# A hybrid S5 / short-convolution / expert-retrieval step on one core: the front's DVE and TensorE orders, its loads, and the latents' query weights rearranged

## The reference

```python
sh1, sc1, g1, sh2, sc2, g2 = modulation(cond)                # silu(cond) @ w_mod + b_mod, once for each of the two conditions
h = rmsnorm(x, norm1_g) * (1 + sc1) + sh1
u, cb, cc, ch = split(h @ w_in)
y_ssm  = gelu(s5_scan(u, forward) + s5_scan(u, backward) + d_skip * u); y_ssm *= sigmoid(y_ssm @ w_glu + b_glu)
y_conv = cb * short_conv(cc * ch)                            # width 3
x = x + g1 * (concat(rmsnorm(y_ssm), rmsnorm_by_head(y_conv)) @ w_out)
h = rmsnorm(x, norm2_g) * (1 + sc2) + sh2
for each block of 128 tokens, for each of 8 heads:
    q = h @ w_query[head]                                    # 256 columns
    s = q halves @ sub_keys                                  # 2 x 128 scores for a token
    idx, top = 16 best of the sums of the 16 best of each half
    out += (gelu(expert_u[idx] . h) * softmax(top)) @ expert_v[idx]
x = x + g2 * out;  y = rmsnorm(x, final_norm_g)
```

## Time and profile before

| | |
|---|---|
| median of 3 runs | 1988.73 us (1987.07 to 1994.5) |
| the profiled execution's own time | 1987.85 us |
| its span | 1986.1 us |
| busy PE / DVE / ACT / POOL | 1201.5 / 1443.9 / 375.6 / 736.0 us |
| moved by DMA | 745.90 MB, 671.13 of them by POOL's queue |
| first expert row set issued at | 234.18 us |

### The profile page before, as it was taken

How to read it: one execution, slowest core, us unless ns; L and a number is a source line. 1 busy time by engine, 2 the same in 40 slices (tenths; PEclk the granted TensorE clock), 3 DMA queues, 4 the chain that set the end, 5 groups by cost and what they waited for, 6 DMA issues and landing times.

```text
span 1986.1 us, 22255 instructions
## 1 busy us (share of the span) xinstructions
PE 1201.5 (60%) x7540; PEld 465.5 (23%) x7540; DVE 1443.9 (73%) x3889; ACT 375.6 (19%) x845; POOL 736.0 (37%) x673
## 2 busy tenths in 40 slices
PE   5988988888867666666544443364344454444444
PEld 2557733333322222222111000021000011111001
DVE  8778367877766776766788777777777767877675
ACT  4241342122222221111111110121011111211110
POOL 3100132333433333343443444444444444344442
PEclk8999989999968877777655555575555556555555
DMA  8556499999989999999999999999999999999996
GB/s 337 170 186 209 155 394 383 358 394 389 395 339 390 382 393 394 401 403 388 421 421 420 415 417 413 421 407 414 416 415 420 409 414 410 416 421 404 415 414 258
DMA packets 126098, 745.90 MB, mean 376 GB/s; under 512 B 12112, under 2 KB 34896, under 8 KB 40352
## 3 DMA queue, kind: packets, MB, share of 16 engines
q0 software_dynamic: 92160, 671.13, 82.8%
q1 hardware_dynamic: 33824, 73.35, 10.5%
HBM read 741.78 MB, written 2.65 MB: 375 GB/s over the span
## 4 chain that ended last, share of the span: by engine, by line
DMA 31%; PE 29%; DVE 26%; issue 10%; ACT 2%; POOL 0%; DVEq 0%; POOLq 0%; SPq 0%; ACTq 0%
DMA r<-table,gidx 30%; DVE r L1675 8%; PE bank L843 7%; PE bank L811 6%; PE bank L920 3%; PE bank L931 2%; DMA r<-w_query 1%; DVE wgt L1687 1%; PE bank L778 1%; DVE r L1643 1%; DVE i L1617 1%; PE bank L539 1%; PE bank L638 1%; DVE i L1623 1%; DVE r L1618 1%
## 5 line engine op out<-in xcount | busy, mean ns | idle before, releaser
L1875 POOL DMA_INDIRECT r<-table,gidx x640 | 708.9, 1108 | 1063.9 <-PE bank L843 902.6
L1675 DVE CUSTOM_DVE_ANT_0 r<-r 128x1024 f32<-128x1024 f32 x640 | 779.9, 1224 | 310.9 <-DMA r<-table,gidx 292.3
L843 PE MATMUL bank<-r,wgt 128*32 128x512 f32 x2560 | 536.6, 923 | 727.7 <-DVE wgt L1687 709.0
L843 PEld LDWEIGHTS bank<-r,wgt 128*32 128x32 f32 x2560 | 61.4, 130 | 1102.7 <-DVE wgt L1687 1032.2
L1223 ACT ACTIVATE r<-r 128x2 f32<-128x2 f32 x320 | 65.1, 203 | 1045.7 <-DVE r L1675 1042.8
L811 PE MATMUL bank<-hT_r,r 128*128 128x512 f32 x256 | 120.4, 625 | 0.9 <-ACT hT_r L1079 0.9
L1684 DVE TENSOR_TENSOR r<-r 128x2 f32<-128x2 f32 x320 | 50.2, 157 | 82.0 <-ACT r L1223 82.0
L1687 DVE TENSOR_TENSOR wgt<-fold,r 128x64 f32<-128x64 f32 x320 | 72.0, 225 | 11.1
L811 PEld LDWEIGHTS bank<-hT_r,r 128*128 128x128 f32 x256 | 50.3, 202 | 75.9 <-issue 75.9
L1223 ACT ACT_TABLE_LOAD x51 | 65.4, 1283 | 0.9
L920 PE MATMUL bank<-hT_r,r 128*128 128x512 f32 x128 | 62.9, 636 | 0.0
(11 more groups left out here) (362 smaller groups left out, 1472.6 us busy)
## 6 DMA issues: line engine op xcount, KB each, us to landing
r<-w_mod SPq DMA_DIRECT2D x24, 1024.0 KB, 7.8
r<-w_query SPq DMA_DIRECT2D x15, 1024.0 KB
r<-table,gidx POOLq DMA_INDIRECT x640, 11.6
r<-w_tiles SPq DMA_DIRECT2D x12, 512.0 KB, 8.1
x_r<-w_tiles SPq DMA_DIRECT2D x10, 512.0 KB, 4.9
hT_r<-xT SPq DMA_DIRECT2D x4, 640.0 KB, 6.3
r<-w_u SPq DMA_DIRECT2D x1, 2048.0 KB, 31.3
r<-w_o SPq DMA_DIRECT2D x1, 2048.0 KB, 10.5
```

The source lines that it names most:

```text
L843: last = mm(bank[ACC[b % 2][h]][to:to + TG, :], wgt[:, g % 2, e, :], rows[:, k % SLOTS, D + h * 512:D + (h + 1) * 512], start=(G % HEADS = ...
L1675: V.tensor_tensor_reduce(rows[:, s, 0:D], rows[:, s, 0:D], h2r[tg], 1.0, 0.0, ALU.mult, ALU.add, hid[:, par, k:k + 1]).then_inc(dot_done, 1)
L1875: G_.indirect_dma_start(rows[:, k % SLOTS, :], None, table, bass.IndirectOffsetOnAxis(gidx[:, e, k:k + 1], 0)).then_inc(row_in[k % SLOTS], 16)
```

## The change

It moves work in the front and gives the latents' query weights another load and PE another order.

- `bcs` is loaded in two halves: B ahead of the slabs, C (semaphore `ld_cc`) behind `w_u`.
- DVE: `chunk_inputs(0)` goes ahead of the norm's inversion, the gains go between the fourth and fifth scaled tile, and all eight groups of CP are DVE's. POOL's group of CP is gone, and its Bd copies wait for CP.
- PE: turns 0 to 3 go between the slabs 5, 6 and 7, turns 4 to 7 behind the second u tile (turns 4 to 7 stood behind the fifth). Slabs 20 and 21 go behind the two halves of L625, slab 22 ahead of the context's outputs. ACT takes turns 0 to 3 out ahead of the modulation rows.
- DVE's lag blocks come one scan step earlier.
- SP: the first two convolution tiles use the two buffers that the gate's weights need, so that the gate's weights are loaded after two tiles and not after six; the first query's weights go behind two tiles, and `w_o` goes ahead of the last two.
- Latents' queries: `load_query` ends with context head 7. `load_query_lat(n)`, n = 0 and 1, loads the weights of four heads at once as eight loads of 512 KB (one for each k, pieces of 4 KB) into `wq4`, spread over pairs by waits on the count of gelus. `query_lat` of heads u = 9 to 15 is cut in quarters of four matmuls, behind the pairs g = 2, 3 (h = 0) and 4, 5 (h = 1), the scores behind g = 6; for u = 8 whole halves go behind g = 5 and 6 and the scores ahead of g = 7. ACT's copies follow the gelus of g = 4 and 6 (u = 8: 6 and 7), and g = 7 for the scores.

```diff
             def load_conv_ctx(q):
                 if q >= 6:
-                    sp.wait_ge(zc_mm, (1, 2, 3, 4, 7, 8)[q - 6])
+                    sp.wait_ge(zc_mm, q - 3)
...
+            def load_query_lat(n):
+                if n:
+                    sp.wait_ge(lq_mm, HEADS)
+                for k in range(KD):
+                    if n == 0 and k:
+                        sp.wait_ge(gelu_done, NPR * (HEADS - 3) + 6 + k)
+                    elif n and k % 2 == 0 and k:
+                        sp.wait_ge(gelu_done, NPR * (HEADS + 1) + 6 + k // 2)
+                    sp.dma_start(wq4[k // KS][:, k % KS, :], w_query[:, k, 4 * DQ * n:4 * DQ * (n + 1)]).then_inc(ld_wq0, 16)
...
+                if n == 46:
+                    sp.wait_ge(zol_mm, KD)
+                    sp.wait_ge(q_mm, HEADS)
+                    load_query_lat(0)
+            sp.wait_ge(out_ready, 1)
+            sp.dma_start(y_out[:, :, 0:P], peer.rearrange("p (k t) -> p k t", k=KD)).then_inc(out_dma, 16)
+            load_query_lat(1)
...
+                elif h == 0:
+                    pe.wait_ge(ld_wq0, 16 + 16 * KD * (n + 1))
...
-                    if HEADS <= u < NQC:
-                        if g in (4, 5):
-                            query_lat(u, g - 4)
+                    if u == HEADS and g == 7:
+                        scores_lat(u)
+                    add_rows(G, g)
+                    if u == HEADS:
+                        if g in (5, 6):
+                            query_lat(u, g - 5, range(KD))
+                    elif HEADS < u < NQC:
+                        if g in (2, 3, 4, 5):
+                            query_lat(u, g // 4, range(4 * (g % 2), 4 * (g % 2) + 4))
                         if g == 6:
                             scores_lat(u)
-                    add_rows(G, g)
...
                     if HEADS <= u < NQC:
-                        if g in (4, 5):
-                            take_q_lat(u, g - 4)
-                        if g == 6:
+                        if g in ((6, 7) if u == HEADS else (4, 6)):
+                            take_q_lat(u, int(g > 4 + 2 * (u == HEADS)))
+                        if g == 7:
                             take_scores_lat(u)
```

More of the change, by code:

```diff
@@ L395, in _ @@
                 sp.dma_start(hT[:, 2 * j:2 * j + 2, :], xT[:, 2 * j:2 * j + 2, :]).then_inc(ld_x[j], 16)
-            sp.dma_start(bcs, bc).then_inc(ld_bc, 16)
+            sp.dma_start(bcs[:, 0:2], bc[:, 0:2]).then_inc(ld_bc, 16)
             for n in range(8):
@@ L399, in _ @@
             sp.dma_start(wu, w_u).then_inc(ld_wu, 16)
+            sp.dma_start(bcs[:, 2:4], bc[:, 2:4]).then_inc(ld_cc, 16)
             sp.dma_start(dsk[0:NCH, :], dskip).then_inc(ld_dsk, 16)
@@ L406, in _ @@
             sp.wait_ge(d_mm, 1)
-            for q in range(4):
+            for q in range(2, 6):
                 load_conv_ctx(q)
             sp.wait_ge(us_mm, 2)
-            for q in range(4, 6):
+            for q in range(2):
                 load_conv_ctx(q)
@@ L413, in _ @@
                 load_mod(n)
-            for q in range(6, 10):
+            sp.wait_ge(zc_mm, 2)
+            for j in range(2):
+                sp.dma_start(wt[:, j, :, :], w_tiles[NCONV + j]).then_inc(wtg_in, 16)
+            for q in range(6, 8):
                 load_conv_ctx(q)
@@ L417, in _ @@
             sp.dma_start(wqa, w_query[:, :, 0:DQ]).then_inc(ld_wq0, 16)
[L418 to L421, removed]
+            for q in range(8, 10):
                 load_conv_ctx(q)
@@ L424, in _ @@
             sp.dma_start(woA, w_o[:, 0:4, :, :]).then_inc(ld_woa, 16)
+            for q in range(10, 12):
+                load_conv_ctx(q)
             sp.wait_ge(zc_mm, 10)
@@ L462, in _ @@
                     load_out_lat(n - 30)
-                if n % NPR == 5:
+                if n % NPR == 5 and n // NPR + 3 < HEADS:
                     load_query(n // NPR + 3)
[L465 to L469, removed]
+                if n == 46:
[5 more added lines that the diff above has]
+            load_query_lat(1)
             for b in range(1, NBLK - 1):
@@ L533, in turn_input @@
                 last.then_inc(bpt_mm, 1)
+            pe.wait_ge(silu_done, 1)
+            for n in range(KD):
+                mod_slab(n)
+                if n in (5, 6):
+                    turn_input(2 * (n - 5))
+                    turn_input(2 * (n - 5) + 1)
+            mod_turn(0)
             def u_lat(k):
@@ L558, in _ @@
                 mod_slab(KD + k)
-                if k in (1, 4):
-                    for e in range(4):
-                        turn_input((0 if k == 1 else 4) + e)
+                if k == 1:
+                    for e in range(4, 8):
+                        turn_input(e)
             pe.wait_ge(bpt_ev, 7)
@@ L627, in _ @@
                 last.then_inc(m_mm, 1)
[L628 to L629 removed]
+                mod_slab(20 + a)
+            mod_slab(22)
             def conv_ctx(r):
@@ L809, in query_lat @@
                     pe.wait_ge(topk_done, u)
-                for k in range(KD):
-                    last = mm(bank[2 + h][:, :], wqb[:, k, h * P:(h + 1) * P], hT[:, k, CTX:T], start=(k == 0), stop=(k == KD - 1))
-                last.then_inc(lq_mm, 1)
+                for k in ks:
+                    last = mm(bank[2 + h][:, :], wq4[k // KS][:, k % KS, at:at + P], hT[:, k, CTX:T], start=(k == 0), stop=(k == KD - 1))
+                if ks[-1] == KD - 1:
+                    last.then_inc(lq_mm, 1)
             def scores_lat(u):
@@ L1100, in mod_take @@
                       bank[6 + h][:, CW:CW + 16].rearrange("p (m a c) -> p a m c", m=MCH, a=4), ACT.Copy).then_inc(mod_free, 1)
+            for e in range(4):
+                take_input(e)
             mod_rows(0)
@@ L1108, in _ @@
                 modulate(0, k, 1, CTX, T).then_inc(h_ready, 1)
-            for e in range(8):
+            for e in range(4, 8):
                 take_input(e)
@@ L1426, in _ @@
             V.tensor_copy(sv[:, 9, :], sv[:, 4, :]).then_inc(bb_ready, 1)
-            dve.wait_ge(rms_act, 2)
-            link(V.reciprocal(rs, rs))
-            for k in range(KD):
-                tt(hT[:, k, :], hT[:, k, :], rs, ALU.mult).then_inc(xs_ready, 1)
             def chunk_inputs(n):
@@ L1455, in _ @@
             chunk_inputs(0)
-            gains(1, COL_N1, 2)
+            dve.wait_ge(rms_act, 2)
+            link(V.reciprocal(rs, rs))
+            for k in range(KD):
+                if k == 4:
+                    gains(1, COL_N1, 2)
+                tt(hT[:, k, :], hT[:, k, :], rs, ALU.mult).then_inc(xs_ready, 1)
             for n in range(1, 4):
@@ L1460, in _ @@
             ct = tv.rearrange("p (q j c) -> p q j c", q=4, j=Q + 1)
-            for q4 in range(CP_POOL, NQ, 4):
+            dve.wait_ge(ld_cc, 16)
+            for q4 in range(0, NQ, 4):
                 q = slice(q4, q4 + 4)
```

55 lines of the change are left out of this document (14 added, 41 removed).

## The result

The changed kernel takes **1999.75 us** (median, 1998.43 to 2002.36) against 1988.3 us for the kernel before (1987.07 to 1994.5) in the same session: ratio **1.0049, interval 1.003 to 1.0069**. The forecast was 1966 us, range 1952 to 1984. The change is slower, by about as much as a measurement of this kernel can just tell, and the forecast missed by 34 us. The profiled execution has a span of 1998.8 us.

What follows compares the result with a forecast made beforehand. It took a PE, DVE and ACT relay to bound the front until 234 us, then the DMA engines: 1987.85 - 13.8 (front) - 8.8 (queries) = 1965.2, plus 0.9 for the median, 1966 us; range 1952 to 1984.

Steps and rivals of the forecast that it cites:

- The front: All before the first expert row set, a relay between PE, DVE and ACT: -10.1 - 3.7 = -13.8 us; ends -7 and -17.
- (a) to (c): Front: u starts 4.5 us sooner, PE reaches chunk states at 102.6, CP ready at 98.6, first copy out 10.1 us sooner.
- (e): Gate weights loaded after two tiles: PE's 2.81 us wait goes, L713 starts 3.8 us sooner; -3.7 us.
- The load of 8 MB in 4 KB pieces: Latents' query weights: 2.7 us for 1 MB against 3.1 in 1 KB pieces; eight heads gain 3 us.
- late loads: Rival: PE's first latent query waits for its group's loads, stopping POOL and DMA; 2007 us if landing takes 29.7; chance 0.06.
- the row that priced it at 29.7 us: Profile row of the load at 397.84, in 1 KB pieces, which took 29.67 us and held PE up.
- a wait for `w_query` of more than 3 us: Sign named in advance that the prediction is wrong: PE waiting this long for the query weights.
- The step of u = 8: First latents' query step, keeping whole bursts: loses 9.6 us in place of 5.1, 4.5 us later than now.
- The 16.0 us of waiting: Rest of the 8 latents' query steps, 365.4 - 324.6 - 8 x 3.1; forecast to fall to 13.1 us.
- 324.6 us of row sets: The 8 latents' query steps at 40.6 us each for 16 row sets, the base before loads and waiting.
- ACT's wait: Latents' query steps: ACT's gelu stands behind PE's burst, DVE waits 32.2 us in 11 times; quarters end it.
- 171 forecast: DMA engines: price in ns of one 4 KB piece, so 2.7 us for 1 MB.

Runs made afterwards that it cites:

- e1: The changed kernel's front alone, with the query loads, PE's query order and ACT's takes of the kernel before; 1978.27 us, ratio 0.995.
- e3: The changed kernel with its four-head loads, but PE's whole query bursts and ACT's copies in the places of the kernel before; 1989.12 us, ratio 0.9997.
- e4: The changed kernel with no gelu waits in the second group's loads and y_out stored behind them; 1991.71 us, ratio 1.0022.
- e6: Against e1: no loads of the latents' query weights, the queries use head 7's (output not the reference's); 1973.52 us, ratio 0.9927.
- e7: Against e1: latents' queries of two matmuls for a half instead of eight, loads kept (output not the reference's); 1955.93 us, ratio 0.9848.
- e9: Against e1: both no loads of the latents' query weights and two matmuls of eight for each query half; 1939.58 us, ratio 0.9756.
- e8: Against e1: one-head 1 MB loads into two buffers in turn, all latents' queries in quarters, ACT's takes one pair later; 1973.41 us, ratio 0.9925.
- e5: The changed kernel with the first group's eight loads issued in one go and u = 8's query in quarters; 1995.15 us, ratio 1.0035.
- e10: Against e8: from u = 9, each query's first half moved behind pairs 7 and 0, weights loaded one head further ahead; 1966.89 us, ratio 0.9891.

## Why the prediction was wrong

- *The front*: (a) to (c) right: 4.45 us at u (4.5), 7.5 at the chunk states (6.8), CP at 98.1 (98.6), the first copy out 10.6 sooner (10.1). DVE's scan behind it starts even 12.0 sooner, 114.99 in place of 126.94, because before, PE still had 96 of its 128 matmuls to do after that copy, and now it goes straight through. (e) is too large: PE's wait for the gate weights is gone, but it now waits 6.35 us behind the gate for ACT, and the output projection starts at 181.36 in place of 194.10, 12.7 sooner. So (e) gave under 1 us and not 3.7. The first row set is 12.8 sooner for 13.8 because the two errors nearly cancel. In the medians e1 shows 9.9 of it, 6.8 to 12.9. Timelines of DVE and PE after:

```profile
114.99 0.20 DVE L1539 COPY fin<-r 128x64 f32<-128x64 f32 x1 [9.28 <-ACT r L1168]
170.98 1.84 PE L691 MATMUL bank<-ones,mix_r 128*128 128x1 f32 x8 [6.35 <-ACT mix_r L1193]
181.36 2.02 PE L763 MATMUL bank<-mix_r,r 128*128 128x128 f32 x16 [0.76 <-issue]
```

- *The load of 8 MB in 4 KB pieces.* The step that failed: I took the landing of one 512 KB load, 9.1 us, for that of the last of eight. A single load does land in that time (8.64 us in e3's chain); the last of eight queued within 13 us lands in 29.24 in the changed kernel (32.20 in e4, where they are queued within 4), and q1 has little over a quarter of the engines meanwhile. I had the right rival, late loads with a threshold of about 20 us, and the row that priced it at 29.7 us, and gave it 0.06. I put that row aside because it was in 1 KB pieces; it would have given the right time for the second group. By that rival both groups would be late; the first is paced over 36 us in place of 13, its last load lands like a lone one, and it was late only in e3. Of the 41 us that the rival had for both groups, one wait of 15.21 us came; it is also the sign that I had named, a wait for `w_query` of more than 3 us. And I had no term at all for four heads' weights in one step: e3 shows some 7 us of it.
- *The step of u = 8*: I had it 4.5 us longer, it was 9.2. Ahead of it the head start is 10.9 us, and 14.5 in e1, but that is no price of the loads: e6, which loads no weights for the latents, has 8.7. Of this, 3.6 us arise between the spreads at about 408 and 460 us, where the programs of e1 and e6 are the same, and a context query waits 2.59 us for its weights and then runs at 3.52 us in e6, 1.51 and 2.05 in e1. So profiled executions of one program differ by some 6 us at 550 us, and sums of steps are to be read with the starts beside them.
- *The 16.0 us of waiting, and the bytes as a sum.* This step failed too, and would have without any late load. The 8 steps are not 324.6 us of row sets plus loads plus waits that can be taken off one by one; they are a relay of 44.4 us beside which row sets and one load, 43.7 us by my prices, run nearly hidden. Taking ACT's wait away (32.2 us in 11 times, 12.8 in 6 after) shortened the last three steps by nothing, since PE's run is as long in quarters as in bursts. e6, e7 and e9 show this; e8 sizes the quarters at 5 us or less.
- *Sum*: forecast -22.6; measured -9.9 for the front and about +21.5 for the queries (1999.75 - 1978.27).

What stays open: how the 9.2 us at u = 8 divide between the first group's bytes, its paced loads and the burst order, since each experiment there let another wait through (e3 the load, e5 the latents' input). What sets the 30 us of a queued group, pieces, bytes or `y_out` ahead of it, stays open as well. That e10's 1966.89 us are the number of the forecast is a coincidence: it got there by another program.

## What to carry to other kernels

Beside a saturated stream from another queue, price a load from a row in which as much was queued with it, not by the landing of a lone one; and where PE's in-order list holds that wait, give the load that time or make it smaller. Spread loads evenly over steps that an engine relay sets: a step with four of them is longer, and the steps without any are not shorter. Before bytes and waits are added up for a step, follow the chain through one whole step: if no DMA stands in it, the loads are free up to the slack, and only shortening the run on the chain pays. Work on that run can move into the gaps of the same engine's other phase, as in e10.

## What the runs showed of the hardware

Beside the row sets, 1 MB in 1024 pieces of 1 KB took 29.67 us, and 4 MB in 1024 pieces of 4 KB took 35.5 us from the first issue to the last landing (e4): larger pieces carried four times the bytes in nearly the same time. A lone load of 512 KB took 8.64 us (e3), and a row set 17.29 us while a group was going through (e3), with a median of 11.2 before. In the engines' share the pieces cost near what I had worked out: 27.2% of 16 x 40 us for e4's 1388 packets is 174 us, and if the 364 others cost 48.5 ns each, it is 153 ns for a piece of 4 KB, an estimate (171 forecast). The granted clock was 0.50, the level of 1.2 GHz, in e3 and e4 from 740 to 760 us, after PE had idled 3 to 5 us ahead of each pair; and in the chain of after the first quarter of the run took 5.57 us in place of 3.63. That is 1.9 us of the relay of 44.4. The quarters behind it ran at 3.63 us, with one pair between them: the short bursts did not bring the lower clock back.
